# Block turns by VectorE and a trip through DRAM for 12 of the 16 head-output tiles of the first layer

## What is computed

```python
h = rmsnorm(x, norm_gain[l]) * (1.0 + scale[:, None, :]) + shift[:, None, :]
proj = h @ w_in[l]
...
y_a = att.reshape(B, S, D_A) * jax.nn.silu(g_a)
...
y_b = head_groupnorm(ret, ret_norm_gain[l]).astype(x.dtype) * jax.nn.silu(g_b)
y = jnp.concatenate([y_a, y_b], axis=-1) @ w_out[l]
x = x + gate[:, None, :] * y
```

## Time and profile before

| | before |
|---|---|
| median of 3 runs | 1823.51 us (1823.32 to 1823.84) |
| the profiled execution | 1823.72 us |
| span of its trace | 1821.8 us |
| TensorE busy | 1795.9 us (99%) |
| VectorE busy | 1325.8 us (73%) |
| ScalarE busy | 966.8 us (53%) |
| GpSimd busy | 180.6 us (10%) |
| mean granted TensorE clock | 0.998 |

### The profile page before, as it was taken

How to read it: one execution, slowest core, us unless ns; L and a number is a source line. 1 busy time by engine, 2 the same in 40 slices (tenths; PEclk the granted TensorE clock), 3 DMA queues, 4 the chain that set the end, 5 groups by cost and what they waited for, 6 DMA issues and landing times.

```text
span 1821.8 us, 25060 instructions
## 1 busy us (share of the span) xinstructions
PE 1795.9 (99%) x9653; PEld 1465.2 (80%) x9653; DVE 1325.8 (73%) x1881; ACT 966.8 (53%) x1373; POOL 180.6 (10%) x232
## 2 busy tenths in 40 slices
PE   7999999999999999999999999999999999999998
PEld 3568788888888878888888888888888888888887
DVE  6349989998986888657777644588886466776665
ACT  5335565456456446544654644477774444444564
POOL 1000021001000000210000000044431020110001
PEclk9999999999999999999999999999999999999999
DMA  9999979976986976656377655855555555678762
GB/s 358 389 369 348 307 252 337 318 238 215 348 296 207 383 259 233 231 162 208 123 261 253 220 200 185 289 174 181 165 184 185 187 185 183 197 241 311 248 226 93
DMA packets 207635, 444.01 MB, mean 244 GB/s; under 512 B 8096, under 2 KB 23340, under 8 KB 206380
## 3 DMA queue, kind: packets, MB, share of 16 engines
q1 hardware_dynamic: 192124, 414.15, 66.5%
q10 hardware_dynamic: 15408, 28.47, 4.3%
HBM read 428.41 MB, written 14.17 MB: 243 GB/s over the span
## 4 chain that ended last, share of the span: by engine, by line
PE 91%; DVE 4%; DMA 2%; ACT 1%; issue 1%; SPq 0%; POOLq 0%; ACTq 0%; POOL 0%; DVEq 0%
PE acc L875 27%; PE acc L877 27%; PE acc L876 27%; DVE w_lo L2251 1%; PE tps L1014 1%; DMA raw<-in_w_in 1%; DMA raw<-in_w_mod 1%; DMA proj<-in_w_mod 1%; PE acc L1053 0%; PE acc L1055 0%; PE acc L1054 0%; PE sps L1053 0%; PE sps L1152 0%; DVE proj L2439 0%; PE sps L1151 0%
## 5 line engine op out<-in xcount | busy, mean ns | idle before, releaser
L2251 DVE TENSOR_TENSOR w_lo<-raw,w_hi 128x1024 fp32r<-128x1024 f32 (+1 forms) x572 | 712.2, 1250 | 382.7 <-ACT w_hi L1488 379.7
L1488 ACT ACTIVATE w_hi<-raw 128x1024 fp32r<-128x1024 f32 (+1 forms) x572 | 599.1, 1051 | 720.5 <-PE acc L877 633.5
L875 PE MATMUL acc<-w_hi,ht_hi 128*128 128x512 f32 (+1 forms) x2256 | 887.0, 393 | 0.8 <-issue 0.8
L877 PE MATMUL acc<-w_hi,ht_lo 128*128 128x512 f32 (+1 forms) x2256 | 874.8, 388 | 0.0
L876 PE MATMUL acc<-w_lo,ht_hi 128*128 128x512 f32 (+1 forms) x2256 | 873.3, 387 | 0.0
L877 PEld LDWEIGHTS acc<-w_hi,ht_lo 128*128 128x128 f32 x2256 | 423.4, 188 | 87.8
L875 PEld LDWEIGHTS acc<-w_hi,ht_hi 128*128 128x128 f32 x2256 | 423.6, 188 | 87.0 <-issue 4.0
L876 PEld LDWEIGHTS acc<-w_lo,ht_hi 128*128 128x128 f32 x2256 | 424.0, 188 | 82.2
L2439 DVE SCALAR_TENSOR_TENSOR proj<-raw,vcol,proj 128x1024 f32<-128x1024 f32 x60 | 80.2, 1337 | 3.8
L2439 DVE SCALAR_TENSOR_TENSOR scr<-raw,vcol,scr 128x1024 f32<-128x1024 f32 x60 | 79.0, 1316 | 4.3 <-DVE w_lo L2251 0.5
L3228 POOL TENSOR_TENSOR scr<-scr 128x128 f32<-128x128 f32 x56 | 31.1, 587 | 324.8 <-DVE scr L2931 324.8
(11 more groups left out here) (365 smaller groups left out, 1510.3 us busy)
## 6 DMA issues: line engine op xcount, KB each, us to landing
raw<-in_w_in SPq DMA_DIRECT2D x203, 1024.0 KB, 5.1
raw<-in_w_mod SPq DMA_DIRECT2D x64, 1024.0 KB, 5.9
raw<-in_w_out SPq DMA_DIRECT2D x32, 1024.0 KB, 5.6
raw<-in_w_mod SPq DMA_DIRECT2D x44, 512.0 KB, 11.4
raw<-in_w_o SPq DMA_DIRECT2D x16, 1024.0 KB, 5.9
raw<-in_w_ple_gate SPq DMA_DIRECT2D x16, 1024.0 KB, 5.2
proj<-blocks ACTq DMA_DIRECT2D x17, 512.0 KB, 6.1
raw<-in_w_b_out SPq DMA_DIRECT2D x8, 1024.0 KB, 5.1
```

The costliest lines, as they stand in the source:

```text
L875: pe.matmul(o, hi_m, w_hi[:, slot, u, 0:width], start=start, stop=False)
L877: mm = pe.matmul(o, lo_m, w_hi[:, slot, u, 0:width], start=False, stop=stop)
L1488: act.activation(w_hi[:, x % SPL, :, 0:width], raw[:, j, 2 * (x % halves):2 * (x % halves) + 2, 0:width], ACT.Copy).then_inc(hi_ready, 1)
L2251: dve.tensor_tensor(w_lo[:, x % SPL, :, 0:width], raw[:, j, 2 * (x % halves):2 * (x % halves) + 2, 0:width], w_hi[:, x % SPL, :, 0:width]. ...
```

## The change

Layer 0 takes the way of layer 1. Three trips are added for it, `o_first`, `o_second`, `o_third`, in three more blocks of DRAM (23 for 20); since layer 0 still uses `scr` for the attention's bias, they are staged in `proj`. `o_second` is turned at half 2 of chunk 12 like `y_second`, but `o_first` at half 8 (layer 1: 4), and its DMAs are issued at halves 10 and 12 (layer 1: 6 and 8), as its buffer is that of `o_second`. `o_third` is as in layer 1. TensorE keeps pairs 6 and 7. The counts that others wait for (`turned`) are adapted.

```diff
-        blocks = nc.dram_tensor("blocks", (20, P, 1024), F32, kind="Internal").ap()
+        blocks = nc.dram_tensor("blocks", (23, P, 1024), F32, kind="Internal").ap()
...
+        o_second = trip(proj[:, 0, QI:QI + 1024], proj[:, 1, QI:QI + 1024])
+        o_first = trip(proj[:, 0, QI:QI + 1024], proj[:, 0, QI:QI + 1024], after=o_second)
+        o_third = trip(proj[:, 0, QB:QB + 1024], proj[:, 1, QB:QB + 1024])
...
+        layer_outputs = ((o_first, o_second, o_third), (y_first, y_second, y_third))
...
-                if l == 0:
-                    gemm(1, chunk_halves(1), 8, at=(l, 14), width=TAIL, side=last_retention(l))
-                else:
-                    gemm(1, chunk_halves(1), 8, at=(l, 14), width=TAIL, side=lambda t, x, first: retention(l, 16 + x))
+                gemm(1, chunk_halves(1), 8, at=(l, 14), width=TAIL, side=lambda t, x, first: retention(l, 16 + x))
+                turned_in_memory(12)
...
+                y_first, y_second, y_third = layer_outputs[l]
+
                 def first_retention(t, x, first):
                     if x == 1:
                         probs_columns()
                     retention(x)
-                    if l and x == 4:
+                    if x == 4:
                         to_memory(y_second)
-                    if l and x == 6:
+                    if x == 6:
                         from_memory(y_second)
+                    if x == (6 if l else 10):
                         to_memory(y_first)
-                    if l and x == 8:
+                    if x == (8 if l else 12):
                         from_memory(y_first)
...
                 def last_retention(t, x, first):
                     retention(16 + x)
-                    if l == 0:
-                        early_tiles(x, 0, False, of_outputs(l))
-                        return
                     if x == 6 or x == 7:
                         memory_pair(y_first, 2 * x - 12, 2 * x - 12)
...
                 def outputs_and_gates(t, x, first):
-                    if l == 0:
-                        early_tiles(x, None, True, of_outputs(l))
-                    else:
-                        outputs_from_memory(x)
+                    outputs_from_memory(x)
...
                 def last_outputs(t, x, first):
                     if x == 3:
                         outputs(GA + 2 * HD)
                     retention(x)
-                    if l and x == 2:
+                    if x == 2:
                         dve.wait_ge(y_ready, 2 + NH * l + 4)
                         turn_blocks(y_second, in_blocks(proj, GA + 4 * HD, CH))
-                    if l and x == 4:
+                    if x == (4 if l else 8):
                         dve.wait_ge(y_ready, 2 + NH * l + 8)
                         turn_blocks(y_first, in_blocks(proj, GA, CH))
...
                 def last_retention(t, x, first):
                     retention(16 + x)
-                    if l == 0:
-                        early_tiles(x, 0, False, of_outputs(l))
-                        return
                     if x == 5:
                         dve.wait_ge(yg_ready, NH // 2 * l + 2)
                         turn_blocks(y_third, in_blocks(proj, VB, CH))
...
                 def outputs_turned(t, x, first):
-                    if l == 0:
-                        early_tiles(x, None, True, of_outputs(l))
-                        return
                     if x == 0 or x == 1:
                         memory_pair(y_second, 2 * x, 2 * x + 4)
```

More of the change, by code:

```diff
@@ L1266, in output_columns @@
                 return proj[:, m, col:col + HD]
-            def last_retention(l):
-                turned_early = early_side(0, output_columns, gated_outputs(l))
-                def side(t, x, first):
-                    retention(l, 16 + x)
-                    turned_early(t, x, first)
-                return side
             def embedding_turned(t, x, first):
@@ L1314, in _ @@
                 else:
-                    turned_in_memory(12)
                     gemm(1, chunk_halves(2), 8, ready=early_ready, side=late_side(output_columns, gated_outputs(l)))
@@ L2306, in layer_scaled @@
                 if p % 2:
-                    dve.wait_ge(turned, 2 + KT + 2 * p + 2)
+                    dve.wait_ge(turned, 2 + 4 + 2 * p + 2)
                     if p >= 2:
@@ L3207, in _ @@
                     pool.tensor_tensor(y, y, gb, ALU.mult).then_inc(yg_ready, 1)
-                xfree.skip(KT)
+                xfree.skip(4)
                 accs.skip(4)
```

## The result

| | before | after |
|---|---|---|
| median | 1823.63 us (4 runs, 1823.32 to 1823.84) | 1834.91 us (4 runs, 1834.27 to 1835.37) |
| the profiled execution, its span | 1823.72, 1821.8 us | 1834.83, 1833.0 us |
| mean granted TensorE clock | 0.998 | 0.997 |

The account below looks back on a forecast made before the run. TensorE, 91% of the chain that ended last, was taken as the bound, losing time wherever VectorE makes it wait. Terms -2.65 + 4.04 + 1.1 = +2.5 us gave 1826.0 us, range 1820.8 to 1828.4 us.

Parts of the forecast that it names:

- What is taken away: Layer 0's tail: TensorE loses six of eight pairs of transposes, 0.44 us a pair, -2.65 us.
- The two turns: Chunks 12 and 13 of layer 0: VectorE's two turns of 2.02 us delay TensorE's masked scores, +4.04 us.
- Chunk 15: Layer 0: pairs 4 and 5, made behind two modulation pieces, come late for TensorE, +1.1 us, bounds 0.1 to 2.9 us.
- Chunks 16 and 17: Layer 0: costed at nothing, because VectorE gets back in step in chunk 15's halves 4 to 7.
- rival 2: VectorE's backlog of chunk 15 is carried through full chunks 16 and 17: about 1828.6 us, chance 0.19.
- Sum of layer 0: Tail gain, two turns and chunk 15 together: -2.65 + 4.04 + 1.1 = +2.5 us.

Follow-up runs that it names:

- e4: Kernel before plus only VectorE's two turns beside chunks 12 and 13 of layer 0, written where nobody reads, no trips, all transposes kept; 1828.08 us.
- e5: Changed kernel with the kernel before's DRAM places, one modulation piece moved from chunk 12 to chunk 18 of layer 0; 1826.57 us.
- e9: Changed kernel with old DRAM places, layer 0's first two turns moved behind half 15 of chunks 12 and 13 and into the tail, trips later; 1826.11 us.
- e2: Changed kernel with the kernel before's DRAM blocks for all trips both have, the three new trips in the last three blocks; 1828.05 us.
- e7: Changed kernel with only the mix stage's pair of 256 KB trips back at its old DRAM places, by exchange; 1832.19 us.
- e8: Changed kernel with old DRAM places for its trips, except the mix stage's pair at its new blocks 17 and 18; 1828.40 us.
- e11: Changed kernel with old DRAM places, but the mix stage's third trip at its new block 16 in exchange for block 13; 1833.29 us.
- e13: Changed kernel with only the mix stage's third trip back at its old block 13 in exchange for block 16; 1828.02 us.
- e18: Changed kernel with old DRAM places, but the mix stage's third trip at block 19 in exchange for block 13; 1827.93 us.
- e12: Changed kernel with the mix stage's trips at old DRAM places, earlier trips at new ones, four hg trips at places of neither kernel; 1828.07 us.
- e3: Changed kernel in which VectorE turns one 32 by 32 block instead of sixteen in each of layer 0's six pieces; 1829.90 us.
- e1: Kernel before with every trip's DRAM block three places further, nothing else added; 1825.25 us.
- e14: Kernel before with the mix stage's third trip at block 16 in exchange for block 13, array of 23 blocks; 1826.58 us.
- e6: Changed kernel with old DRAM places, layer 0's first two turns moved to half 13 of chunks 12 and 13 and half 3 of the tail; 1827.27 us.

## Why the prediction was wrong

- **What is taken away, -2.65 us: right.** 16.08 us for the tail, in every kernel with three trips in which VectorE wasn't behind. The price read from layer 1 held to 0.01 us.
- **The two turns, +4.04 us: right**, mechanism and size. The three waits grew from 1.03 us to 2.79 + 1.69 + 0.61 = 5.09 us, by 4.06 us; the stage lost 4.35 us. e4 shows that it is the turns by themselves, e5 and e9 that it is VectorE's missing idle time at that place.
- **Chunk 15, +1.1 us: mechanism right, too small.** It measured 2.41 us, inside this term's bounds of 0.1 to 2.9 us. The forecast let the two pieces and pair 4 share one slowing by GpSimd, at the 1.05 us that layer 1 shows (2.18 against 1.13 us). In the changed kernel it fell on two `w_lo`, 4.54 us instead of 2 x 1.22 us, so 2.1 us, while pair 4 took 1.13 us and the pieces 2.60 and 2.61 us. Counted from the end of the tail, pair 4 was done 463.49 - 450.44 = 13.05 us later instead of layer 1's 923.65 - 915.87 = 7.78 us: 5.27 us more against 4.26 us in the forecast. The step that was off is to take the size of the slowing from the instruction on which it fell in layer 1. The Trainium skill, "SBUF — State Buffer", section "Who interferes with whom", says that a VectorE instruction with two inputs in SBUF contends with a GpSimd instruction that reads SBUF. The trace agrees: both inputs of `w_lo` are in SBUF, and two of them took 4.54 instead of 2.44 us beside GpSimd's products.
- **Chunks 16 and 17, nothing: right; chunk 18, not in the sum: 1.04 us.** Chunks 16 and 17 gained 0.01 us of shift. Behind them the profiled execution lost 1.04 us by one wait for `w_lo` at 532.7 us; others with the same layer 0 lost 0 to 0.8 us (e2, e7, e8, e11 to e13, e18). The prediction had named a new wait for `w_lo` behind 470 us as the sign of rival 2, and this is one, but not by rival 2's mechanism: VectorE was back in step at the start of chunk 16, and lost its time anew in chunks 17 and 18 by weights that landed later. Why they land later in some executions stays open.
- **Sum of layer 0**: +2.5 us were forecast, 4.1 to 5.2 us came. Without the loss of the second block the changed kernel takes 1828.0 us (e2, e12, e13), inside the range and just under rival 2's 1828.6 us.
- **The missing term, +6.4 us: the step that failed.** The sum has no term for anything behind layer 0, which puts the second block at nothing, and no reason is given. I never asked, of the trips after layer 0, how much margin each has, nor noted that the three added blocks move all of them in DRAM. The trace of before had the warning: `mix_pairs`' tiles are done 2.3 us before TensorE needs them, on a write and a read of 6.0 us together. In the changed kernel these took 12.1 us, TensorE stood for 3.3 us, and with the lower clock behind it that cost 6.37 us. No rival held this, so the range left it out.
- **All together.** The 11.3 us are the forecast's 2.5 us, 0.3 us more at the masks, 1.3 us more in chunk 15, 1.0 us behind chunk 17 and 6.4 us in the second block, less 0.2 us at the start.

What is shown: the place of one trip decides how often the loss comes (e2, e12 and e13 against e3, e7 and e11; e2 and e3 ran on one chip, e11 and e12 on another), and neither the moment nor the place of the slow pair does. What stays open: why block 16, and by what path the place of one 512 KB trip leaves one DMA engine 2.3 us behind at the next. With the six added DMAs and the new place all four executions of the changed kernel and all six of e3 took over 5 us more than their layer 0 accounts for (e3: 1828.7 to 1830.5 us, where layer 0 ends 0.4 us ahead of the kernel before); with the new place alone, in e1 and e14, only a part of the executions did or came near it. But e7 and e11 have both as well, and one execution each took only 1829.0 and 1827.7 us. What part the added DMAs have was not tried by itself, and not all kernels ran on the same chip.

## What to carry to other kernels

Work that is moved to an engine with 97 to 98% busy time in a stage is paid there in full, unless it goes where that engine waits; waits of the bound engine hide a backlog, so removing one moves part of the cost to the next place (e9: 4.35 us saved at the masks, 2.2 us lost again in chunk 15, of which 1.3 us is a longer wait and most of the rest the lower clock). A small change that only shifts buffers in DRAM can cost more than its own work: list each round trip through DRAM with its margin, and take one with 2.3 us in hand on a 6 us trip as a risk for the range, and look which other DMA is issued next to its read. Compare a loss in a stage that the change doesn't touch first with the same kernel at the old addresses; it is one line.

## What the runs showed of the hardware

- A DRAM write and read of 256 KB took 6.0 us together, or 12.1 us, in the same stage of the same program; where an earlier buffer lay in DRAM decided how often the long case came. In it some 2.3 us passed with about one packet in flight, and the read, issued 1.2 us behind 1 MB of weights instead of 1.0 us ahead of them, took 6.85 instead of 2.91 us.
- After 3.3 us of standing still, TensorE's granted clock fell from its full 2.4 GHz to its lower level, 1.2 GHz, for some 6 us (matmuls 0.43 us apart instead of 0.23 us), which cost 2.9 us on top of the wait. In e14 a wait of 3.8 us cost 1.6 us more. A wait of 2.8 us at the first mask left the clock at 1.00 in the changed kernel, e4, e8 and e13; in e7, e11, e12 and e18 it fell, and in e2 it was 0.79 over 388 to 404 us, where TensorE lost 2.9 us beyond the wait. In e6 it fell behind a wait of 2.15 us. In e2 that cost nearly nothing in the end: the next two masks were then ready, and chunks 12 and 13 lost 4.43 us instead of 4.35 us.
